# Four head means of the HGRN stage from a rounded part and its rest, and eight scalings of the residual rows at other places of the vector engine's order, in a two-block fp32 kernel

## The reference, cut to what matters

```python
def rms_norm(x, g):
    return x * lax.rsqrt(jnp.mean(x * x, axis=-1, keepdims=True) + EPS) * g

x = rms_norm(h_of_first_block, final_norm_g)      # the residual rows, scaled
proj = rms_norm(x, norm1_g) @ w_in                # queries, keys, values, ...
q, k = rms_norm(heads(q_sb), q_norm_g), rms_norm(heads(k_sb), k_norm_g)
o_sb = stick_breaking_attention(q, k, heads(v_sb))
o = rms_norm(hgrn_scan(...), hg_norm_g) * silu(g_in)   # four heads, mean over 128
h = x + (sigmoid(gate_sb) * (o_sb @ w1) + sigmoid(gate_hg) * (o @ w2)) @ w_out
```

## Time and profile before

| what | value |
|---|---|
| median of 3 runs | 1366.21 us (1364.23 to 1367.04) |
| the profiled execution, its own time | 1363.15 us |
| its span in the trace | 1361.7 us |
| granted TensorE clock | 1.0 of full speed |
| TensorE busy | 1353.5 us, 99% of the span |
| VectorE busy | 878.3 us, 64% |
| ScalarE busy | 822.3 us, 60% |
| GpSimd busy | 333.7 us, 25% |

### The profile page before, as it was taken

How to read it: one execution, slowest core, us unless ns; L and a number is a source line. 1 busy time by engine, 2 the same in 40 slices (tenths; PEclk the granted TensorE clock), 3 DMA queues, 4 the chain that set the end, 5 groups by cost and what they waited for, 6 DMA issues and landing times.

```text
span 1361.7 us, 19658 instructions
## 1 busy us (share of the span) xinstructions
PE 1353.5 (99%) x7510; PEld 1135.6 (83%) x7510; DVE 878.3 (64%) x1612; ACT 822.3 (60%) x1275; POOL 333.7 (25%) x306
## 2 busy tenths in 40 slices
PE   9999999999999999999999999999999999999999
PEld 6977966789899898887777878888888898889889
DVE  6055466578576673357698789975437785568557
ACT  6575566663544535666588677775656645754553
POOL 0211101235343251111211111211113261315214
DMA  7976643925426137877765575668888546824733
GB/s 244 243 167 143 149 117 77 229 36 189 106 87 184 30 134 188 189 167 153 154 139 122 131 199 124 138 143 182 201 215 202 111 138 175 184 47 161 189 53 109
DMA packets 57971, 202.46 MB, mean 149 GB/s; under 512 B 6451, under 2 KB 7020, under 8 KB 57749
## 3 DMA queue, kind: packets, MB, share of 16 engines
q0 software_dynamic: 25632, 93.09, 36.6%
q1 hardware_dynamic: 31380, 106.24, 23.6%
q10 hardware_dynamic: 864, 1.87, 0.4%
HBM read 199.05 MB, written 2.12 MB: 148 GB/s over the span
## 4 chain that ended last, share of the span: by engine, by line
PE 90%; DVE 3%; ACT 3%; DMA 3%; POOL 1%; issue 1%; SPq 0%; ACTq 0%; POOLq 0%; DVEq 0%
PE bank L644 22%; PE bank L651 22%; PE bank L648 22%; PE bank L682 15%; PE bank L840 2%; PE bank L816 2%; PE bank L830 1%; PE bank L797 1%; DMA WH<-in_w_in 1%; PE bank L865 1%; DMA RAW<-in_w_in 1%; ACT WH L1010 0%; DMA WL<-in_w_in 0%; POOL quarters_s L2185 0%; ACT WL L1018 0%
## 5 line engine op out<-in xcount | busy, mean ns | idle before, releaser
L644 PE MATMUL bank<-NH,WH 128*128 128x512 f32 x1152 | 460.5, 401 | 0.3 <-ACT NH L1191 0.2
L648 PE MATMUL bank<-NL,WH 128*128 128x512 f32 x1152 | 448.3, 390 | 0.5 <-DVE NL L1454 0.5
L651 PE MATMUL bank<-NH,WL 128*128 128x512 f32 x1152 | 448.2, 390 | 0.6 <-DVE WL L1449 0.5
L644 PEld LDWEIGHTS bank<-NH,WH 128*128 128x128 f32 x1152 | 216.1, 188 | 61.5 <-issue 18.8
L651 PEld LDWEIGHTS bank<-NH,WL 128*128 128x128 f32 x1152 | 216.3, 188 | 47.4 <-DVE WL L1449 0.9
L648 PEld LDWEIGHTS bank<-NL,WH 128*128 128x128 f32 x1152 | 216.3, 188 | 44.6 <-DVE NL L1454 2.8
L1010 ACT ACTIVATE WH<-RAW 128x1024 fp32r<-128x1024 f32 (+3 forms) x148 | 151.9, 1031 | 75.1 <-PE bank L651 38.3
L682 PE MATMUL bank<-AH,WH 128*128 128x256 f32 x644 | 182.6, 284 | 0.5 <-DVE gains_hT L1831 0.3
L682 PE MATMUL bank<-AL,WH 128*128 128x256 f32 x644 | 182.2, 283 | 0.0
L682 PE MATMUL bank<-AH,WL 128*128 128x256 f32 x644 | 182.2, 283 | 0.0
L1018 ACT ACTIVATE WL<-WH 128x1024 fp32r<-128x1024 f32 (+1 forms) x146 | 153.2, 1051 | 16.2 <-DMA WH<-in_w_in 13.9
(11 more groups left out here) (375 smaller groups left out, 2139.2 us busy)
## 6 DMA issues: line engine op xcount, KB each, us to landing
WL<-in_w_in POOLq DMA_DIRECT2D x58, 512.0 KB, 6.5
RAW<-in_w_gu SPq DMA_DIRECT2D x44, 512.0 KB, 5.4
WL<-in_w_gu POOLq DMA_DIRECT2D x34, 512.0 KB, 7.8
RAW<-in_w_ff SPq DMA_DIRECT2D x32, 512.0 KB, 4.8
WH<-in_w_in POOLq DMA_DIRECT2D x32, 512.0 KB, 6.3
RAW<-in_w_in SPq DMA_DIRECT2D x28, 512.0 KB, 6.3
quarters<-in_w_ff SPq DMA_DIRECT2D x24, 512.0 KB, 4.8
WL<-in_w_ff POOLq DMA_DIRECT2D x17, 512.0 KB, 6.4
```

The lines of the kernel that those rows point to most:

```text
L644: e.matmul(o, a[0], a[1], start=(k == 0), stop=False)
L648: e.matmul(o, b[0], b[1], start=False, stop=False)
L651: mm = e.matmul(o, c[0], c[1], start=False, stop=(k == t.kt - 1))
```

## The change

It has three parts. The head means: ScalarE also rounds the square (`mean_high` into `sq1`, seen as `sq_r[1]`), VectorE writes the rest (`mean_low` into `hn0`, seen as `hn_r[0]`), and TensorE multiplies both in fp32r instead of the one fp32 product. The order around them: TensorE's mean is planned one unit later, ScalarE's root half a unit later. The scalings: their eight planned times become 7, 9, 11, 13, 21, 29, 60 and 68 units after `T_DS` instead of 32, 38, ..., 74.

```diff
@@ build_program @@
-        sq_r, gt_r, zb_r, eb_r = rounded("sq", 2), rounded("gT", 2), rounded("zb", 2), rounded("eb", 2)
+        sq_r, gt_r, zb_r, eb_r, hn_r = rounded("sq", 2), rounded("gT", 2), rounded("zb", 2), rounded("eb", 2), rounded("hn", 1)
@@ tensor, hgrn_sums @@
                     sum_values("hg_sum", vH, h, ATh[h % 2])
-                    yield h_time(8 * h + 11, 1.7)
+                    yield h_time(8 * h + 11, 2.7)
                     bank, free = take("hg_mean", h)
-                    pe.wait_ge(("hg_square", h), *free)
-                    e.matmul(bank, ones1k, hn[0], start=True, stop=True).then_inc(*pe.sig("hg_mean", h))
+                    pe.wait_ge(("mean_low", ("hg", h)), *free)
+                    mean_of(bank, ones_r[0], sq_r[1], hn_r[0]).then_inc(*pe.sig("hg_mean", h))
@@ scalar, hgrn, norms @@
                         e.activation(hn[0], OB, ACT.Square).then_inc(*act.sig("hg_square", h))
-                        yield h_time(8 * h + 12, 1.7)
+                        mean_high(("hg", h), hn[0], sq_r[1], ("hg_square", h))
+                        yield h_time(8 * h + 12, 2.2)
                         root_act(("hg", h), bank_of("hg_mean", h), hn[1], ("hg_mean", h), unit=8.0)
@@ vector, root_second @@
                 for k in range(8):
-                    yield T_DS + 32 + 6 * k
+                    yield T_DS + (7, 9, 11, 13, 21, 29, 60, 68)[k]
                     dve.wait_ge(lo("n_second", k), ("dve_root", "second", 3))
@@ vector, hgrn, norms @@
                         key, bank = ("hg", h), ("hg_mean", h)
+                        yield h_time(8 * h + 11, 2.1)
+                        mean_low(key, hn[0], sq_r[1], hn_r[0])
                         yield h_time(8 * h + 13, 1.7)
                         root_square(key, hn[1], hn[2])
```

## The result

The changed kernel takes 1370.3 us (median of 6 runs, 1369.15 to 1373.35), the kernel before 1366.31 in the runs beside it (median of 6). By these medians it is slower by 4.0. The ratio on record, which is not the quotient of the medians, is 1.0039, with a 95% interval of 1.0029 to 1.0049: slower by 5.3 us, between 4.0 and 6.7. The prediction said 1370.2 and slower by 4.0. The profiled execution of the change took 1369.35, its span is 1368.0.

What follows compares the result with a forecast made beforehand. TensorE, busy 99%, was taken to bound the kernel, except in about 50 us of norms where the chain runs through roots and scalings. Norms +1.3 and head means +2.7 gave +4.0 on 1366.21: 1370.2, range 1365.8 to 1372.8.

Steps and rivals of the forecast that it cites:

- The scalings: Query and key norms: first root +0.6, scalings inside two roots +0.65 each, one removed from the chain -0.65; about +1.3.
- the sixth scaling: Inserted on VectorE inside the first query row's root, on the chain: +0.65.
- TensorE's waits in the norms: Key means: first wait about as long as before, new wait of about 0.6 at the last; TensorE has slack there.
- The saving of the means: Four head means: rounded part and rest take 0.46 instead of fp32's 0.87; four times 0.42 saves 1.7.
- The waits of heads 0 to 2: TensorE waits for VectorE's rest (L955) at these heads' means: 0.5, 0.7 and 0.
- the last task of head 0: Its operands, ready at 852.80, move to 854.05 with TensorE there at about 853.8: +0.3.
- The fourth head: Head 3's mean: new ScalarE rounding delays VectorE's read-out and rest, so TensorE waits 2.5, plus a restart of 0.1.
- The sum: Whole kernel: norms +1.3, head means +2.7 (waits and restarts 4.4 less 1.7 saved), +4.0; forecast's chance 61%.
- Only the norms and the first two heads pay: Rival: the last head's rest is not late, so 2.5 + 0.1 fall away; +1.4, 1367.6; 24%.
- The faster one: Rival: first query root not late, sixth and seventh scalings fit into pauses, rests in time; -2.4, to 1363.5; 8%.
- The closed pipe: Rival: VectorE shut behind each instruction, scalings or rests cost 1.2, root at 623.03 about 3 late; about +9, 1375; 2%.
- The late weight piece: Rival: later ScalarE weight work or a load in other traffic makes TensorE wait; +2 to +4 more, 1373; 5%.

Runs made afterwards that it cites:

- e7: Kernel before with all eight scalings in VectorE's idle time around the fourth query read-out, fp32 head means kept; ratio 1.0008 to the kernel before.
- e8: Kernel before with five scalings in idle time around the fourth query read-out, the other three at the change's places; ratio 0.9999 to the kernel before.
- e5: Kernel before with all eight scalings ahead of the first three query read-outs, fp32 head means kept; ratio 1.0016 to the kernel before.
- e3: The change's head means with the scalings as before, means, roots and rests replanned so that no mean waits; ratio 0.9987 to the kernel before.
- e9: The change with the fourth head's mean three products later on TensorE, nothing else; ratio 1.0022 to the kernel before.
- e2: The change's head means alone, scalings at the places of before; ratio 1.0026 to the kernel before.
- e11: The change unaltered, run once more for a second profile; ratio 1.0036 to the kernel before.
- e6: The change with the fourth head's mean six products later on TensorE, nothing else; ratio 1.0025 to the kernel before.
- e10: The change with the fourth head's mean twelve products later on TensorE and its root on ScalarE behind it; ratio 1.0008 to the kernel before.
- e4: The change's head means replanned so that no mean waits, and all eight scalings in VectorE's idle time among the norms; ratio 0.9982 to the kernel before.
- e1: Kernel before with only the scalings at the change's places, fp32 head means kept; ratio 1.0002 to the kernel before.

## Why the prediction was right, and which term of it was not

**The scalings.** Predicted +1.3, measured +0.99. The first root is 0.45 late (0.6 said), the sixth scaling costs 0.54 (0.65 said), since it takes part of the step between L925 and L929. The one at 638.79 that is gone gives back 0.52 (e7; 0.65 said), which leaves 0.52 for the seventh (0.65 said). The terms are those of the sum, each a little smaller; e8 shows that the four ahead cost 0.44, and e5 that the first root's lateness is the delay of the read-outs less a fixed 2.0.

**TensorE's waits in the norms.** Predicted "about as long as before" at the first key mean and a new one of 0.6 at the last. Found: 1.23 instead of 0.86 by starts, and 0.63 instead of 0.06. Both cost nothing of their own; TensorE has slack there, as was said.

**The saving of the means.** 0.42 for each said, 0.43, 0.44, 0.43 and, in the stretch of the fourth, 0.30 found in e3. The products stand 0.23 apart throughout; the 131 ns of the Trainium skill ("TensorE: Matmul & The Clock Gate", section on the back-to-back issue gap) would have made heads 0 and 2 save 0.6 each, an estimate from that figure, and no trace here does.

**The waits of heads 0 to 2.** Predicted 0.5, 0.7 and 0, found 0.46, 0.68 and 0; the last task of head 0 0.40, with 0.3 said. From 814.3 to 900.7 the change loses 0.71; the terms of the sum give 1.5 + 0.3 for restarts - 1.26 = +0.54.

**The fourth head.** The wait was predicted at 2.5 and is 2.5 in the profile, 2.63 by starts. Here the sum is wrong in size: it priced what TensorE loses at the wait itself and a restart of 0.1, 2.2 with the saving, and 3.9 was lost. Of the missing 1.7, 1.6 is the granted clock at half behind the wait, 0.2 in each of eight spacings, and 0.1 the longer wait. The spacing of the mean itself, 0.34 instead of 0.23, is the restart that the sum has; it is the same in e9, where the clock held. The sum took the clock behind the wait as full without saying so. e2 and e11 show the fall again, e6, e9 and e10 show that it goes with the wait.

**The sum.** 0.99 + 0.13 (up to 814.3) + 0.71 + 3.91 + 0.39 behind the stage = 6.13 in the profiled execution, where +4.0 was said. The norms came out 0.3 under, the clock took 1.6 that the sum does not have, and the rest, 0.8, is the longer wait, the slightly dearer first heads and two stretches that the sum leaves out. By the medians the change costs 4.0, as forecast; by the ratio 5.3, with 4.0 at the edge of the interval. That the forecast of 1370.2 met the median of 1370.3 so closely is partly luck: a cost of 1.6 is missing from the sum, and the change's own run to run spread is 4 us. Direction, places and the waits are right for the reasons given, the norms' terms a little too large; the clock was not among the terms. The bounds have a small slip: the sum's upper bounds, +1.3 and +5.5, give 1373.0, a little beyond the 1372.8 at which the range ends.

**The rivals.** "Only the norms and the first two heads pay" would have come out as e10 did (+1.1; +1.4 was said); rows 13 were the reason against it, and ScalarE's rounding did hold the rest up. The faster one fell at the point where it decides: the first root is 0.45 late, with none of the 0.49 of idle ahead of it left, and the sixth and seventh scaling cost 0.5 each. The closed pipe fell by the same two figures, against its 3 and 1.2. The late weight piece did not bring the change's time, but it is real in other executions.

## What to carry to other kernels

A rest of a square belongs in VectorE's list where its rounded part is ready, and the reader a few products behind it; price the reader's wait by what stands ahead of the rest on VectorE and what that waits for in turn. A wait of some 2 us or more on TensorE can cost more than its length: look at the granted clock in the stretch behind it, and try moving the reader by a few products, which here gave 2.3 us for 0.7 of wait. What is put ahead of a read-out is free up to the slack of the engine that reads next (2.0 us here) and is paid in full beyond it.

## What the runs showed that I had not expected

**The clock falls behind some waits and not behind others, and their length alone does not decide.** By starts: it fell behind 2.63, 2.63 and 2.62 (change, e2, e11), behind 2.43 in e8, and behind 1.82 in e7; it did not behind 1.98 (e5), 1.94 (e9) and 1.92 (e4). TensorE in e7, a wait for a piece of weight:

```profile
672.15 0.40 PE L648 MATMUL bank<-NL,WH 128*128 128x512 f32 x1
674.20 0.71 PE L651 MATMUL bank<-NH,WL 128*128 128x512 f32 x1 [1.65 <-DMA WL<-in_w_in]
674.70 0.63 PE L644 MATMUL bank<-NH,WH 128*128 128x512 f32 x1
```

and its stretches, and those of e5, where the clock held:

```profile
673.00:674.00 1.00, 0.00 (x0) 0.00 (x0) 0.00 (x0) 0.00 (x0) 0.00 (x0) 1.00 0.90 209
...
675.00:676.00 1.00, 1.00 (x4) 0.72 (x4) 0.00 (x0) 0.21 (x1) 0.00 (x0) 0.50 0.99 205
```

```profile
633.00:635.40 2.40, 0.70 (x4) 0.24 (x2) 2.33 (x5) 0.44 (x1) 0.00 (x0) 1.00 0.94 195
635.40:636.50 1.10, 0.98 (x4) 0.84 (x5) 0.88 (x3) 1.07 (x3) 0.00 (x0) 1.00 0.25 48
```

In each fall the clock came back within some 4 us, at a cost of 1.3 to 1.7. By their mean clocks, two runs of e11 and three of e2 had no such fall either. What else decides it is open; no run was made on that alone.

**Two weight loads set much of the spread between executions.** The small product near 814 (L865) waits at the end of a chain that begins with a load into `WH`. The chain of the kernel before, and that of e8:

```profile
797.29 9.28 DMA WH<-in_w_in
...
814.27 0.68 PE bank L865 x4
```

```profile
798.60 10.61 DMA WH<-in_w_in
...
816.90 0.84 PE bank L865 x4
```

The waits by starts are 1.11 and 2.43. In all fourteen traces this wait is the load's time less 8.17 us, within 0.02, with loads from 8.97 to 10.61. At 672 the like holds for the load into `WH` and the one into `WL` behind it, in the eleven traces whose chain goes through both: 12.66 together in the kernel before for a wait of 0.32, 13.59 for 1.22 in e1, 14.17 for 1.82 in e7, the sum less 12.35 each time, within 0.04. Loads of the same bytes that differ by 1.5 us, at two places, and a fall of the clock behind the longest, make nearly 4 us between single profiled executions, as much as the change. It is why e1, e7 and e8 could be told apart only in the traces, from the start of the norms to the first product behind them, and not by their times.
